# A two-block transformer layer on one core: first modulation weights laid out by output tile, seven input products that walk along the tiles of h, buffers moved by 128 bytes, output stored by tiles

## What is computed

```python
mod = c @ w_ada + b_ada                        # w_ada: 1024 x 6144
sh_a, sc_a, gt_a, sh_m, sc_m, gt_m = split(mod, 6)
h = rmsnorm(x, g_mix) * (1 + sc_a) + sh_a
z = h @ w_in                                   # zq, zkc, zvc, zks, zvs, zkw, zvw, zg, zqd, zkvd, zkr, zga, zgb
# compressed, selected and window attention (nsa) on the first eight, latent attention (mla) on the next three
y = sigmoid(zga) * (o_nsa @ w_o_nsa) + sigmoid(zgb) * (o_mla @ w_o_mla)
x = x + gt_a * (y @ w_out)
h = rmsnorm(x, g_mlp) * (1 + sc_m) + sh_m
x = x + gt_m * (relu(h @ w_fc1) ** 2 @ w_fc2)  # 4096 wide
```

## Time and profile before

| | |
|---|---|
| median of three runs | 2230.45 us |
| the profiled execution | 2229.57 us, its span 2227.8 us |
| TensorE busy in the span | 2094.4 us, 94% |
| weight loads of TensorE | 1642.6 us, 74% |
| VectorE, ScalarE, GpSimd busy | 1154.6, 785.7, 731.4 us |
| mean granted clock of TensorE | 0.973 |
| moved by DMA | 186.88 MB, 84 GB/s on the mean |

### The profile page before, as it was taken

One profiled execution on the slowest core, in us unless ns is written; L12 is line 12 of the kernel. 1 busy time (PEld: TensorE's weight loads), 2 busy tenths in 40 slices (PEclk: granted clock), 3 DMA queues, 4 the chain that ended last, 5 costly groups with the idle time before them and its releaser, 6 DMA issues. The chain is left out here.

```text
span 2227.8 us, 35971 instructions
## 1 busy us (share of the span) xinstructions
PE 2094.4 (94%) x14896; PEld 1642.6 (74%) x14896; DVE 1154.6 (52%) x1803; ACT 785.7 (35%) x1292; POOL 731.4 (33%) x347
## 2 busy tenths in 40 slices
PE   6898889999899999989999999999999998999997
PEld 5785566887688888767767777776777786888885
DVE  6426775332652342736678767767713456523322
ACT  2335656223332232442333333333334333322321
POOL 0321020444344444443232233223233443444442
PEclk9989999999999999989999999999999999999998
DMA  7541011533233333331111111111132432333331
GB/s 263 180 140 39 30 48 48 182 121 95 69 101 95 95 95 95 93 106 42 33 44 46 35 33 48 43 35 40 45 110 75 133 95 76 91 95 98 95 95 57
DMA packets 51456, 186.88 MB, mean 84 GB/s; under 512 B 5728, under 2 KB 6880, under 8 KB 50784
## 3 DMA queue, kind: packets, MB, share of 16 engines
q1 hardware_dynamic: 47520, 174.49, 25.1%
q10 hardware_dynamic: 3776, 10.09, 1.3%
HBM read 178.27 MB, written 6.29 MB: 83 GB/s over the span
## 5 line engine op out<-in xcount | busy, mean ns | idle before, releaser
L680 POOL TENSOR_TENSOR wlo<-raw,whi 128x1024 fp32r<-128x1024 f32 x266 | 644.0, 2422 | 1323.7 <-ACT whi L1296 1323.6
L763 PE MATMUL psum<-ah,whi 128*128 128x512 f32 x1288 | 539.0, 419 | 28.1 <-POOL wlo L680 16.6
L764 PE MATMUL psum<-ah,whi 128*128 128x512 f32 x1288 | 512.8, 398 | 0.0
L765 PE MATMUL psum<-ah,wlo 128*128 128x512 f32 x1288 | 511.6, 397 | 0.0
L1296 ACT ACTIVATE whi<-raw 128x1024 fp32r<-128x1024 f32 x266 | 280.1, 1053 | 367.6 <-PE psum L765 304.6
L763 PEld LDWEIGHTS psum<-ah,whi 128*128 128x128 f32 x1288 | 247.3, 192 | 102.5 <-POOL wlo L680 27.0
L765 PEld LDWEIGHTS psum<-ah,wlo 128*128 128x128 f32 x1288 | 247.7, 192 | 55.1
L764 PEld LDWEIGHTS psum<-ah,whi 128*128 128x128 f32 x1288 | 248.1, 193 | 43.6 <-issue 0.2
L2006 DVE SCALAR_TENSOR_TENSOR x<-upad,vec,x 128x512 f32<-128x512 f32 x240 | 210.7, 878 | 5.1
L763 PE MATMUL psum<-hidden,whi 128*128 128x512 f32 x536 | 213.1, 398 | 0.0
L765 PE MATMUL psum<-hidden,wlo 128*128 128x512 f32 x536 | 212.7, 397 | 0.0
(11 more groups left out here) (340 smaller groups left out, 2851.2 us busy)
## 6 DMA issues: line engine op xcount, KB each, us to landing
raw<-in_w SPq DMA_DIRECT2D x322, 512.0 KB, 3.6
x<-in_x SPq DMA_DIRECT2D x1, 2048.0 KB, 8.2
x_kept<-x ACTq DMA_DIRECT2D x1, 2048.0 KB, 9.4
ao_kept<-ao ACTq DMA_DIRECT2D x8, 256.0 KB, 2.2
aof<-ao_kept ACTq DMA_DIRECT2D x1, 2048.0 KB, 12.2
x<-x_kept ACTq DMA_DIRECT2D x1, 2048.0 KB, 9.1
out<-x SPq DMA_DIRECT2D x1, 2048.0 KB, 6.3
lwt<-in_lw ACTq DMA_DIRECT2D x8, 128.0 KB, 2.1
```

Of the source, the lines that this page charges most:

```text
L680: pool.tensor_tensor(wlo[:, s % NHL, :], raw_of(SPLITS[s]), whi[:, s % NHL, :].bitcast(F32), ALU.subtract).then_inc(lo_done, 1)
L763: pe.matmul(dst, wh, h_, start=first, stop=False)
L764: pe.matmul(dst, wh, l_, start=False, stop=False)
L765: return pe.matmul(dst, wl, h_, start=False, stop=last)
```

## The change

The blocks of `ada` 0 and 1 are laid out anew as `("mod", m, half)`: for output tile m, its 128 shift and 128 scale columns, four channel tiles of 128 in each half. VectorE sums them 256 columns wide into one of two sums (`take_mod`), TensorE sums two columns of 128 for each tile (`sum_mod`), and VectorE makes shift and gain of the tile (`mod_tile`). Squares of x are added up on VectorE, and TensorE sums the total once. The spread factor is copied to SBUF, GpSimd multiplies each tile of x by it, and ScalarE applies gain and shift into `tmp`, rounds, and VectorE makes the low half. Seven products of z (`AHEAD`), each in a PSUM bank of its own, take up each tile of h as it comes; the third joins at tile 1, the fourth at tile 2, and so on, and makes up for the tiles it missed. Their weights have seven places, five of them in buffers that are used later for other things. The remaining six `z` come in a new `FRONT`. `ada` 2 stands beside the first eight products behind these seven, `ada` 3 and 4 beside the gates, and `ada` 5 beside `fc1` of chunk 0 of the first MLP, with its sum on TensorE behind the first product of chunk 1. x comes in four transfers, `vec` in two. A buffer `to_line` of 32 floats (128 bytes) that nothing uses is declared behind `modg`. The output is stored tile by tile. The diff, cut to its core:

```diff
-FRONT = [("z", 4), ("z", 5), ("z", 11), ("bkv", 0), ("z", 12), ("bkv", 1), ("ck", 0, 0), ("z", 13), ("ck", 0, 1), ("z", 14), ("ck", 0, 2),
...
+AHEAD = [("z", 11), ("z", 4), ("z", 12), ("z", 5), ("z", 13), ("z", 14), ("z", 15)]
+FRONT = [("z", 10), ("bkv", 0), ("z", 7), ("bkv", 1), ("ck", 0, 0), ("ss", "cq"), ("ck", 0, 1), ("z", 9), ("root", "cq"), ("ck", 0, 2), ("ck", 0, 3),
+         ("z", 6), ("norm", "cq"), ("ck", 1, 0), ("ck", 1, 1), ("z", 8), ("ss", "ckv"), ("ck", 1, 2), ("kc",), ("root", "ckv"), ("ck", 1, 3),
+         ("gt",), ("norm", "ckv"), ("vt", 0), ("vt", 1), ("z", 0), ("vc",)]
...
+    n = Z_LATE.index(f)
+    return [("ada", 2, n)] if n < KT else []
+def begun(m):
+    return min(m + 2, len(AHEAD))
...
-    out = [("raw", ("ada", s, k)) for s in range(2) for k in range(KT)]
+    for m in range(KT):
+        out += [("raw", ("mod", m, half)) for half in range(2)]
+        out += [("split", f) for f in AHEAD[begun(m - 1) if m else 0:begun(m)]]
...
 def mlp_blocks(n):
+            out += [("split", (f"fc{half}", n, c, m))] + ([("raw", ("ada", 5, m))] if (n, half, c) == (1, 1, 0) else [])
...
+def place(s):
+    return s if s < len(AHEAD) else (s - len(AHEAD)) % NHL
...
         modg = sb("modg", [P, 2 * KT])
+        sb("to_line", [P, 32])
...
+                w_ahead2 = sb("w_ahead2", [P, 4, D], F32R, ahead_of)
+                mod_sums = sb("mod_sums", [P, 2, 2 * P], F32, ahead_of)
...
+                    w_ahead = sb("w_ahead", [P, 6, D], F32R, ahead_of)
...
+        spread_x = [qT[:, i, :] for i in range(4)] + [ksd[:, i, :] for i in range(G)] + [kwd[:, i, :] for i in range(G)]
...
         def _(sp):
             sp.dma_start(eye_ones[:, :], io["eye_ones"]).then_inc(const_loaded["eye_ones"], 16)
+            for i in range(KT // 2):
+                sp.dma_start(x[:, 2 * i:2 * i + 2, :].rearrange("p k s -> p (k s)"), x_in[:, 2 * i * S:2 * i * S + 2 * S]).then_inc(x_loaded[i], 16)
+                if i == 2:
+                    sp.dma_start(vec[:, 0:first], vec_in[:, 0:first]).then_inc(vec_loaded, 16)
...
+                    elif old[0] == "mod":
+                        sp.wait_ge(mod_taken, KT * old[1] + 4 * old[2] + 4)
...
-            sp.wait_ge(xn_ready, 2 * KT)
-            sp.dma_start(out.rearrange("p (k s) -> p k s", k=KT), x[:, :, :]).then_inc(stored, 16)
+            for k in range(KT):
+                sp.wait_ge(xn_ready, KT + k + 1)
+                sp.dma_start(out[:, k * S:k * S + S], x[:, k, :]).then_inc(stored, 16)
...
+            wait_emptied(pool, ("rb", "mix"))
+            for m in range(KT):
+                pool.tensor_tensor(spread_x[m], x[:, m, :], sq_sum[:, 1, :], ALU.mult).then_inc(x_scaled, 1)
+                weights_ahead(min(m, len(AHEAD) - 1))
...
+            def sum_mod(m):
+                pe.wait_ge(mod_taken, KT * m + KT)
+                for i in range(2):
+                    mm = pe.matmul(psum[:, OBANK, 2 * m + i:2 * m + i + 1], mod_sum[m % 2][:, i * P:i * P + P], ones[:, 0:1], start=True, stop=True)
+                mm.then_inc(mod_summed, 1)
...
-            sum_squares("mix")
-            ada(0)
+            sum_total("mix")
             spread("mix")
-            ada(1)
+            sum_mod(0)
+            for m in range(KT):
+                had = begun(m - 1) if m else begun(m)
+                for e in range(had):
+                    ahead(e, m)
+                    if e == 1 and m + 1 < KT:
+                        sum_mod(m + 1)
+                for e in range(had, begun(m)):
+                    for k in range(m + 1):
+                        ahead(e, k)
...
                             product(("fc1", n, c, m), ("fc1", n, c, m), ah, range(KT))
+                            if (n, c, m) == (1, 1, 0):
+                                ada(5)
...
+            weights_ahead(0)
+            empty(("rb", "mix"), sq_sum[:, 1, :])
+            weights_ahead(1)
+            for m in range(KT):
+                act.wait_ge(x_scaled, m + 1)
+                act.wait_ge(mod_ready, 2 * m + 2)
...
+                act.activation(tmp[:, n % NTMP, :], spread_x[m], ACT.Identity, bias=mod[:, m:m + 1], scale=modg[:, m:m + 1]).then_inc(pre_split, 1)
+                high(("mix", m), ah[:, 0, m, :])
+                weights_ahead(begun(m + 1) - 1)
...
+            def take_mod(m, k):
+                w, total = raw_of(("mod", m, k // 4))[:, k % 4 * 2 * P:k % 4 * 2 * P + 2 * P], mod_sum[m % 2]
...
+                    ins = dve.scalar_tensor_tensor(total, w, vcol("c", k), total, ALU.mult, ALU.add)
...
+            for k in range(1, KT):
+                add_square("mix", k)
             for k in range(KT):
+                if k == 4:
+                    mean_square("mix", D)
+                take_mod(0, k)
+            inverse_root("mix")
+            for m in range(KT):
+                if m == 0:
+                    mod_tile(m)
+                for k in range(KT if m + 1 < KT else 0):
+                    take_mod(m + 1, k)
+                    if m and k == 1:
+                        mod_tile(m)
+                    if k == 4:
+                        low(("mix", m), ah[:, 0, m, :], ah[:, 1, m, :])
...
                             low(("hid", n, c, m), hidden[c % 2][:, 0, m, :], hidden[c % 2][:, 1, m, :])
+                            if (n, c) == (1, 0):
+                                ada_take(5, m)
+                            elif (n, c, m) == (1, 1, 1):
+                                ada_done(5)
```

More of the change, by code:

```diff
@@ L121, in mlp_blocks @@
 def mlp_blocks(n):
-    return [("split", (f"fc{half}", n, c, m)) for half, c in mlp_order() for m in range(KT)]
+    out = []
+    for half, c in mlp_order():
+        for m in range(KT):
+            out += [("split", (f"fc{half}", n, c, m))] + ([("raw", ("ada", 5, m))] if (n, half, c) == (1, 1, 0) else [])
+    return out
 def parts(what, n):
@@ L265, in bank_order @@
 def bank_order():
-    out = [("ss", "mix"), ("ada", 0), ("rb", "mix"), ("ada", 1)]
+    out = [("ss", "mix"), ("rb", "mix")] + AHEAD
     for f in FRONT:
@@ L887, in attention @@
                         for k in range(k0, k1):
-                            mm = three(bank(what), n % NHL, slice(k * P, k * P + P), ah, k, k == 0, k == KT - 1)
+                            mm = three(bank(what), place(n), slice(k * P, k * P + P), ah, k, k == 0, k == KT - 1)
                         if k1 == KT:
@@ L1273, in _ @@
                         pe.wait_ge(hl_ready, EVENT["early", k] + 1)
-                    mm = three(bank(what), SPLIT_AT[what] % NHL, slice(k * P, k * P + P), hidden[1], k, k == 0, k == KT - 1)
+                    mm = three(bank(what), place(SPLIT_AT[what]), slice(k * P, k * P + P), hidden[1], k, k == 0, k == KT - 1)
                 assert FILL[what] == fills[0], what
@@ L1764, in _ @@
+            for k in range(1, KT):
+                add_square("mix", k)
             for k in range(KT):
-                ada_take(0, k)
-            mean_square("mix", D)
-            for k in range(KT):
-                ada_take(1, k)
-                if k == 2:
-                    inverse_root("mix")
-            ada_done(0)
-            ada_done(1)
-            wait_emptied(dve, ("ada", 1))
-            dve.scalar_tensor_tensor(modg[:, 0:KT], mod[:, KT:2 * KT], 1.0, vcol("g_mix", 0, KT), ALU.add,
-                                     ALU.mult).then_inc(modg_ready, 1)
@@ L1776, in _ @@
-            dve.wait_ge(modg_ready, 1)
-            normalize_tiles("mix", x, lambda k: modg[:, k:k + 1], ah, 0, KT, lambda k: mod[:, k:k + 1])
+                if k == 4:
+                    mean_square("mix", D)
+                take_mod(0, k)
+            inverse_root("mix")
+            for m in range(KT):
+                if m == 0:
[6 more added lines that the diff above has]
+                        low(("mix", m), ah[:, 0, m, :], ah[:, 1, m, :])
+                if m == KT - 1:
+                    mod_tile(m)
+                    low(("mix", m), ah[:, 0, m, :], ah[:, 1, m, :])
@@ L1780, in _ @@
                 if kind == "z":
-                    ada_take(*ada_beside(f)[1:])
-                elif kind == "ada":
-                    ada_done(f[1])
+                    for what in ada_beside(f):
+                        ada_take(*what[1:])
                 elif kind == "bkv":
@@ L2278, in block_of @@
     w_in = w["w_in"]
+    if kind == "mod":
+        m, k0 = what[1], 4 * what[2]
+        parts_of = [w["w_ada"][k * P:k * P + P, s * D + m * P:s * D + m * P + P] for k in range(k0, k0 + 4) for s in range(2)]
+        return np.concatenate(parts_of, 1)
     if kind == "ada":
```

162 lines of the change are left out of this document (97 added, 65 removed).

## The result

The changed kernel takes 2243.24 us by the median of four runs (2241.11 to 2247.57), the kernel before 2229.67 on the same chip. The ratio is 1.0062, 95% interval [1.0043, 1.008]: slower by 13.6 us, more than the 0.2% that a measurement can tell. The forecast was 4 us slower, 2234.5, with a range of 2208 to 2254.

The account below looks back on a forecast made before the run. TensorE, busy 94% of the span, was taken as the bound: its idle stretches and its matmul pace. The terms -14 - 15 + 37 - 4 = +4 gave 2233.6 us, 2234.5 on the median, range 2208 to 2254.

Parts of the forecast that it names:

- The front: Everything before the attention's compressed scores, the mark: start at 158 instead of 172.16 us, -14, bounds +5 and -32.
- The walk: Seven z products taking up h tile by tile: first tile at 33 us, 8.1 a tile, products done at 93.
- at full clock it would be 57, at today's 71; I take 65: Microseconds from the seventh product's end to the attention's start, at TensorE's full clock, at today's, and as forecast.
- The shift: 128 bytes of padding moving `hidden` and the buffers behind `modg`: 0.16 us on each of 103 products, -15, bounds 0 and -18.
- Less where they wait: Deduction from the shift's 103 x 0.16 = 16.5 us for products that wait, leaving -15.
- The rival that the shift does nothing: Slower rival: the 6.7 ns a matmul don't belong to buffer address modulo 256; 2249.5 us, chance 0.18.
- `ada` 5 in fc1: Chunk 0 of the first MLP: `ada` 5's blocks in fc1's ring cost +37 us, bounds 0 and +45 with lower clock.
- The loop: In that fc1, loads wait for takes, takes for `low`, `low` for high halves: 10.3 us a product against 5.44.
- The end: Output stores: eight following the tiles instead of one taking 6.3 us to land; -4 us, bounds -2 and -4.5.
- the lower clock: Slower rival, TensorE at its lower clock: +5 bound in the front, +45 in `ada` 5's part; chance 0.10.
- the quicker walk: Faster rival: GpSimd refilled late, VectorE gets more turns, front up to -32 instead of -14; 2216 us, chance 0.18.
- the cheap ring: Faster rival: waits in fc1's ring misread, `ada` 5 there costs 10 instead of 37 us; 2207 us, chance 0.14.

Follow-up runs that it names:

- noscale: Changed kernel with GpSimd multiplying only 16 of 512 columns of each x tile and ScalarE scaling x itself, h not normalised: 2235.08 us, ratio 1.0015 to the kernel before.
- unshift: Changed kernel without the 128 bytes of padding (`to_line`): 2258.14 us, ratio 1.0116 to the kernel before.
- offsets: Kernel before with padding moving hidden 0 by 256 bytes, hidden 1 by 320, `coh` by 32, `aoh` by 96: one run, 2229.79 us beside 2230.95.
- ring1: Changed kernel with each `ada` 5 take one product earlier on VectorE's list, ahead of the hidden tile: 2205.12 us, ratio 0.9873 to the kernel before.
- onestore: Changed kernel with the output stored by one 2 MB transfer after the last tile, as before: 2251.29 us, ratio 1.0087 to the kernel before.

## Why the prediction was right and wrong

The sign was the forecast's, and each of its four mechanisms is there. The size was 8 to 10 us short, by terms that were mis-sized:

- **The front, -14.** The walk came as worked out: first product 34.0 (33 forecast), h whole at 86.9 (88), seven products at 92.4 (93), the takes stretched by GpSimd, which `noscale` shows as the cause of the first tiles' spacing, 7.7 us (8.1). The end of the walk met the forecast in part by luck: the last tile waited 4.66 us for TensorE's sum, which the prediction has nowhere. What failed is "at full clock it would be 57, at today's 71; I take 65": the 65 has no term behind it, its own terms add up to 69 or 70 at today's clock rather than 71, and the stretch behind the walk took 71.4. The idle time moved instead of going (the 5.6 us at 136), and with it came 15.8 us at half the clock. So -8.4 at the mark, in this execution; those of five others with the same front start the attention at 163.9 to 167.1, a gain of 5 to 8. Up to fc1 the kernel gained 3.8 more, 1.5 of it by the shift: the first small matmuls of the attention take 272 ns by the median where they took 344, with a granted clock of 1.00 in its first 26 us where it was 0.84. Together -12.2.
- **The shift, -15.** It measured 12, by the times (0.54%, 6 to 19 us by the intervals) and by the stretches that read these buffers: 1.5 in `oh` and `yh`, 4.4 in the first MLP, 1.2 in `aoh` and `coh`, 5.2 in the second MLP. The 0.16 us a product holds where products follow each other without a wait; the 32 products of `nm`, `wo`, `pr` and `pc` gave 2.7 where 5.1 had been counted. "Less where they wait" had 1.5 in all, and it was 4.5; that waits are the reason is argued, not shown. The rival that the shift does nothing is refuted by `unshift`. In the Trainium skill (SBUF — State Buffer, "SBUF: two separate sides") the 16-byte lines and a TensorE that waits for no other user would have made the term 0; the 5.60 against 5.44 us decides against reading that as a rule on the pace. The prediction counts the bytes 128 off, as `offsets` found. The edit worked all the same, since it rests only on a shift by 128 that puts these buffers on a par with `ah`.
- **`ada` 5 in fc1, +37.** The loop has the links of the prediction, each of which a trace or a run shows, and its turn was 10.2 us by the median (10.3 forecast). The stretch lost 43.0, 38.5 of it by the loop as `ring1` shows. Counted by ScalarE's relu passes, the ninth comes 73.2 us behind the first where it came 42.5, 30.7 late (28.6 by the forecast's steps), and the step from there over the sum to the tenth takes 11.2 us longer than it did (8.8 forecast). One turn took 11.9, and from the sum on TensorE had 0.63 of its clock for 9.5 us. I had put that in the upper bound, +45, and not in the term.
- **The end, -4.** -4.6 in the traces, and 0.25% in `onestore`.

These make -12.2 (the shift's first 1.5 in it), +43.0, -10.8 and -4.6, +15.4 in all, where the spans differ by 12.3. Of the 3.1 us left, 2.8 lie between the end of the first MLP and the mark in the second: 1.3 of them in the product ahead of that mark, 7.1 us instead of 8.4 because less of it ran at the lower clock, the rest in the stage whose length differs by 7 us from run to run; that it has to do with an edit isn't shown. Of what else the prediction gave a chance, the lower clock came, as some microseconds in two places; the quicker walk and the cheap ring did not.

## What to carry to other kernels

When a load is added to a ring of buffers, follow its release all the way round: which instruction frees the buffer, what stands ahead of that on its engine, and whether that in turn waits for a later load of the same ring. If so, the ring brings no more than that stretch of loads a turn, here one pair of blocks, however idle the queue is, and a consumer moved by one instruction, to where it waits for nothing but its own data, undoes it. A gain ahead of a stretch of small matmuls and late blocks may be partly given back there (`noscale`: 5.6 us at the end of the walk, 3.9 at the attention's start): measure it at the mark where that stretch ends. And where buffers or banks are handed out by the order of a list, a reordered list also changes who waits for whose bank.

## What was not expected

TensorE's pace with its operands' places: 226.7 ns a matmul of 512 columns with `hidden` and the weights at a multiple of 256 bytes, 233.3 with `hidden` at 128 or 192 beyond one, and no better at 160 or 224 with the other buffers; and 232 by the median with the moving operand at a multiple and the weights 128 beyond one. And the walk's length: in the profiled executions of kernels with the same front, the last tile's high half starts between 83.5 and 88.7 us, with VectorE's takes at 49.1 to 49.5 us in sum in all of them.
